# One-hot gating on VectorE, a final norm through PSUM, a 256-column last unit and a later norm sum in a two-block transformer kernel

## The reference, cut to what matters

```
def peer_ffn(...):            # first block: 128 x 128 product keys, 8 heads, top 16 each
    gate = softmax(top_s)     # the gate of each chosen (i, j) expert of a token
    act  = gelu(u[expert] . z)
    return sum(gate * act * v[expert])

def second_block(...):
    x = x + rmsnorm_2(y, g_post_mix)          # y: output of the mixing layers
    h = rmsnorm_2(x, g_pre_mlp)
    f = square(relu(h @ w_up)); f = f @ w_down     # 2048 -> 8192 -> 2048
    return x + rmsnorm_2(f, g_post_mlp)
rmsnorm(x, g) = x * rsqrt(mean(x * x) + eps) * g
```

## Time and profile before

| what | value |
|---|---|
| runs of the kernel before | 3310.08, 3315.99, 3294.74 us; median 3310.08 |
| profiled execution, its own time | 3305.67 us |
| its span, first to last instruction | 3303.8 us |
| TensorE busy | 3191.7 us (97%), 18206 matmuls |
| VectorE, ScalarE, GpSimd busy | 66%, 51%, 26% |
| mean granted clock of TensorE | 0.986 of full speed |

### The profile page before, as it was taken

How to read it: one execution, slowest core, us unless ns; L and a number is a source line. 1 busy time by engine, 2 the same in 40 slices (tenths; PEclk the granted TensorE clock), 3 DMA queues, 4 the chain that set the end, 5 groups by cost and what they waited for, 6 DMA issues and landing times.

```text
span 3303.8 us, 46932 instructions
## 1 busy us (share of the span) xinstructions
PE 3191.7 (97%) x18206; PEld 2781.5 (84%) x18206; DVE 2186.3 (66%) x2875; ACT 1681.1 (51%) x2625; POOL 870.7 (26%) x816
## 2 busy tenths in 40 slices
PE   7999989999999999999999998999998999999997
PEld 6788878888888888888888887888887788888886
DVE  7757998764655555564646579898675855555554
ACT  5554457644545444454545645555656444444453
POOL 1332344521313222231313434222342100000003
PEclk9999999999999999999999999999999999999999
DMA  6465546656565656565565554445665455565663
GB/s 211 149 198 181 179 154 217 236 184 211 187 214 186 211 186 214 186 210 186 193 208 185 185 184 140 159 155 184 190 189 170 153 189 189 190 191 189 190 189 127
DMA packets 177709, 615.35 MB, mean 186 GB/s; under 512 B 18128, under 2 KB 34896, under 8 KB 176080
## 3 DMA queue, kind: packets, MB, share of 16 engines
q1 hardware_dynamic: 157824, 572.59, 54.5%
q10 hardware_dynamic: 19664, 39.76, 3.4%
HBM read 593.41 MB, written 18.87 MB: 185 GB/s over the span
## 4 chain that ended last, share of the span: by engine, by line
PE 73%; DVE 16%; issue 4%; ACT 3%; POOL 3%; DMA 1%; ACTq 0%; POOLq 0%; DVEq 0%
PE G L399 48%; PE G L400 24%; DVE lo L995 7%; DVE CV L1291 2%; DVE oneB L1270 1%; POOL tS L1467 1%; ACT hi L627 1%; DVE tS L1001 1%; DVE oneA L1272 1%; ACT oneB L801 0%; DVE ZA L1314 0%; POOL X L1487 0%; POOL acc L1492 0%; ACT tA L634 0%; DMA X<-in_xT 0%
## 5 line engine op out<-in xcount | busy, mean ns | idle before, releaser
L399 PE MATMUL G<-ZA,hi 128*128 128x512 f32 x5120 | 1824.2, 401 | 29.2 <-DVE lo L995 11.3
L995 DVE TENSOR_TENSOR lo<-raw,hi 128x1024 fp32r<-128x1024 f32 x1088 | 1434.6, 1341 | 305.2 <-ACT hi L627 304.7
L400 PE MATMUL G<-ZA,lo 128*128 128x256 f32 x5120 | 1440.5, 281 | 0.0
L399 PE MATMUL G<-ZB,hi 128*128 128x512 f32 x3584 | 1257.2, 396 | 5.7 <-DVE ZB L1279 4.0
L399 PEld LDWEIGHTS G<-ZA,hi 128*128 128x128 f32 x5120 | 970.3, 190 | 261.2 <-DVE lo L995 13.3
L627 ACT ACTIVATE hi<-raw 128x1024 fp32r<-128x1024 f32 x1088 | 1106.5, 1051 | 46.2 <-DMA raw<-in_pv 30.7
L400 PE MATMUL G<-ZB,lo 128*128 128x256 f32 x3584 | 1003.3, 280 | 0.0
L400 PEld LDWEIGHTS G<-ZA,lo 128*128 128x128 f32 x5120 | 975.7, 191 | 0.6
L399 PEld LDWEIGHTS G<-ZB,hi 128*128 128x128 f32 x3584 | 672.7, 188 | 167.8 <-DVE lo L995 3.2
L634 ACT ACTIVATE tA<-G 128x256 f32<-128x256 f32 x560 | 212.5, 380 | 1001.7 <-PE G L400 998.1
L400 PEld LDWEIGHTS G<-ZB,lo 128*128 128x128 f32 x3584 | 676.8, 189 | 0.0
(11 more groups left out here) (264 smaller groups left out, 1383.2 us busy)
## 6 DMA issues: line engine op xcount, KB each, us to landing
raw<-in_pu SPq DMA_DIRECT2D x256, 512.0 KB, 3.6
raw<-in_pv SPq DMA_DIRECT2D x256, 512.0 KB, 3.6
raw<-in_w_in SPq DMA_DIRECT2D x192, 512.0 KB, 3.6
raw<-in_w_up SPq DMA_DIRECT2D x128, 512.0 KB, 3.6
raw<-in_w_down SPq DMA_DIRECT2D x128, 512.0 KB, 3.5
raw<-in_w_out SPq DMA_DIRECT2D x32, 512.0 KB, 3.5
raw<-in_wq SPq DMA_DIRECT2D x32, 512.0 KB, 3.5
g_scratch<-stage ACTq DMA_DIRECT2D x16, 1024.0 KB, 4.8
```

Of the source, the lines that this page charges most:

```text
L399: pe.matmul(G[:, 0:512], hi[h % NW][:, k % 8, :], Z[:, k, :], start=first, stop=False, skip_group_check=True)
L400: m = pe.matmul(G[:, 0:256], lo[h % NRAW][:, k % 8, :], Z[:, k, 0:256], start=False, stop=last, skip_group_check=True)
L995: dve.tensor_tensor(lo[r][:, :, :], raw[r][:, :].rearrange("p (k n) -> p k n", k=8), hi[w][:, :, :].bitcast(F32), ALU.subtract).then_inc(s ...
```

## The change

Four edits, and a renaming of semaphores: two pairs of semaphores for loads become one each.

1. In `one_hot(k)` VectorE itself multiplies the last four tokens of `oneB` by their gates, right behind `oneA` of the same k. GpSimd's instruction is gone. TensorE's second half of `spread(k)` waits on the new semaphore.
2. In the last unit (u = N-1) the product of `hi` with 512 columns becomes two with 256 columns into the same 256 columns of PSUM, so that one sum holds everything. ScalarE's copy and GpSimd's addition are left out, and VectorE adds Y to the bank directly.
3. At the end ScalarE copies the factor R1 to a PSUM bank, VectorE writes the products to two PSUM banks and adds them to X from there. VectorE has six pieces and GpSimd two.
4. `total` for the norm before the MLP stands behind unit M0+12 and not M0+10, and VectorE forms R3 in step M0+13.

```diff
@@ TensorE, product
-                pe.matmul(G[:, 0:512], hi[h % NW][:, k % 8, :], Z[:, k, :], start=first, stop=False, ...)
+                if u == N - 1:
+                    pe.matmul(G[:, 0:256], hi[h % NW][:, k % 8, :], Z[:, k, 0:256], start=first, stop=False, ...)
+                    pe.matmul(G[:, 0:256], hi[h % NW][:, k % 8, :], Z[:, k, 256:512], start=False, stop=False, ...)
+                else:
+                    pe.matmul(G[:, 0:512], hi[h % NW][:, k % 8, :], Z[:, k, :], start=first, stop=False, ...)
                 m = pe.matmul(G[:, 0:256], lo[h % NRAW][:, k % 8, :], Z[:, k, 0:256], start=False, stop=last, ...)
@@ TensorE, spread
-                        pe.wait_ge(s_ogp, k + 1)
+                        pe.wait_ge(s_ogd, k + 1)
@@ TensorE, loop
-                if u == M0 + 10:
+                if u == M0 + 12:
                     total(2, acc[0], None, (s_rss, 1)).then_inc(s_mean, 1)
@@ ScalarE, evac
-                    low(u)
+                    if u < N - 1:
+                        low(u)
...
                         act.activation(R1[:, :], MB[3][:, 0:256], ACT.Sqrt, ...).then_inc(s_root, 1)
+                        act.wait_ge(s_rcp, 7)
+                        act.activation(MB[2][:, 0:256], R1[:, :], ACT.Copy).then_inc(s_rps, 1)
@@ VectorE, evac
+                if u == N - 1 and part == 1:
+                    dve.wait_ge(s_mm, done(u))
+                    dve.tensor_tensor(Y[:, i, :], GB[BANK[u] % 4][:, 0:256], Y[:, i, :], ALU.add).then_inc(s_join, 1)
-                if st == "dn" and part == 1:
+                if st == "dn" and u < N - 1 and part == 1:
@@ VectorE, one_hot
+                dve.wait_ge(s_ohb, k + 1)
+                dve.tensor_tensor(oB[k % 2][:, 4:8, :], oB[k % 2][:, 4:8, :],
+                                  IJG[:, 2, 8 * k + 4:8 * k + 8].unsqueeze(2).broadcast_to([128, 4, 128]),
+                                  ALU.mult).then_inc(s_ogd, 1)
@@ VectorE, loop (the four instructions that form R3)
-                if u == M0 + 10:
+                if u == M0 + 13:
@@ VectorE, end
-            dve.wait_ge(s_rcp, 7)
-            for n in range(8):
-                k = slice(2 * n, 2 * n + 2)
-                if n not in (1, 4):
-                    dve.tensor_tensor(Y[:, k, :], Y[:, k, :], over(R1, 2), ALU.mult).then_inc(s_fd, 1)
-                if n not in (1, 4, 6):
-                    dve.wait_ge(s_fd, FD_OF[n] - 1)
-                    dve.tensor_tensor(X[:, k, :], X[:, k, :], Y[:, k, :], ALU.add).then_inc(s_fd, 1)
+            dve.wait_ge(s_rps, 1)
+            for n in range(0, len(OUT_D), 2):          # OUT_D = (0, 1, 2, 3, 4, 5)
+                for m in (n, n + 1):
+                    k = slice(2 * OUT_D[m], 2 * OUT_D[m] + 2)
+                    P = MB[m % 2][:, :].rearrange("p (k t) -> p k t", k=2)
+                    if n:
+                        dve.wait_ge(s_fd, m - 1)
+                    dve.tensor_tensor(P, Y[:, k, :], over(MB[2][:, 0:256], 2), ALU.mult).then_inc(s_fm, 1)
+                for m in (n, n + 1):
+                    ...
+                    dve.wait_ge(s_fm, m + 1)
+                    dve.tensor_tensor(X[:, k, :], X[:, k, :], P, ALU.add).then_inc(s_fd, 1)
@@ GpSimd
-                if st == "dn" and c and part == 1:
+                if st == "dn" and c and u < N - 1 and part == 1:
...
-                if 67 <= u < 83:
-                    for k in (2 * (u - 67), 2 * (u - 67) + 1):
-                        pool.wait_ge(s_ohb, k + 1)
...
-                        pool.tensor_tensor(oB[k % 2][:, 4:8, :], oB[k % 2][:, 4:8, :],
-                                           IJG[:, 2, 8 * k + 4:8 * k + 8].unsqueeze(2).broadcast_to([128, 4, 128]),
-                                           ALU.mult).then_inc(s_ogp, 1)
...
-            for n in (1, 4, 6):
+            for m, n in enumerate(OUT_P):              # OUT_P = (6, 7)
                 k = slice(2 * n, 2 * n + 2)
-                if n == 6:
-                    pool.wait_ge(s_fd, FD_OF[6])
-                else:
-                    pool.tensor_tensor(Y[:, k, :], Y[:, k, :], over(R1, 2), ALU.mult).then_inc(s_fp, 1)
-                    pool.wait_ge(s_fp, FP_OF[n] - 1)
+                pool.tensor_tensor(Y[:, k, :], Y[:, k, :], over(R1, 2), ALU.mult).then_inc(s_fp, 1)
+                pool.wait_ge(s_fp, 2 * m + 1)
                 pool.tensor_tensor(X[:, k, :], X[:, k, :], Y[:, k, :], ALU.add).then_inc(s_fp, 1)
```

More of the change, by code:

```diff
@@ L127 @@
 MIX_D = {0: 2, 1: 4, 3: 6, 5: 8, 7: 10}
-FD_OF = {0: 2, 2: 4, 3: 6, 5: 8, 6: 9, 7: 11}
-FP_OF = {1: 2, 4: 4, 6: 5}
+OUT_D, OUT_P = (0, 1, 2, 3, 4, 5), (6, 7)
+OUT_PAIRS = (0, 1, 6, 2, 3, 7, 4, 5)
 TAIL_END = [7, 13, 18, 22]
@@ L254, in build @@
         s_x = [sem(f"s_x{i}") for i in range(4)]
-        s_col, s_con, s_gaw, s_gxw, s_poolw, s_keys, s_mask, s_neg = (
-            sem(n) for n in ("s_col", "s_con", "s_gaw", "s_gxw", "s_poolw", "s_keys", "s_mask", "s_neg"))
+        s_col, s_con, s_gw, s_poolw, s_keys, s_mn = (
+            sem(n) for n in ("s_col", "s_con", "s_gw", "s_poolw", "s_keys", "s_mn"))
         s_st = [sem("s_st0"), sem("s_st1")]
@@ L281, in build @@
         s_sfs, s_sfe, s_sfn = sem("s_sfs"), sem("s_sfe"), sem("s_sfn")
-        s_ohb, s_oha, s_oga, s_ogp, s_spm, s_spr = (
-            sem(n) for n in ("s_ohb", "s_oha", "s_oga", "s_ogp", "s_spm", "s_spr"))
+        s_ohb, s_oha, s_oga, s_ogd, s_spm, s_spr = (
+            sem(n) for n in ("s_ohb", "s_oha", "s_oga", "s_ogd", "s_spm", "s_spr"))
         s_ag, s_gta, s_gl2, s_gm2, s_vx = (
@@ L297, in build @@
             sem(n) for n in ("s_mg", "s_u", "s_yg", "s_pmd", "s_pmp", "s_rsd", "s_rsp", "s_rsq", "s_rss", "s_rn"))
-        s_rl, s_dy, s_yd, s_fd, s_fp = (
-            sem(n) for n in ("s_rl", "s_dy", "s_yd", "s_fd", "s_fp"))
+        s_rl, s_dy, s_yd, s_rps, s_fm, s_fd, s_fp = (
+            sem(n) for n in ("s_rl", "s_dy", "s_yd", "s_rps", "s_fm", "s_fd", "s_fp"))
         def weights(u, p):
@@ L398, in product @@
                 Z = weights(u, p)[1]
-                pe.matmul(G[:, 0:512], hi[h % NW][:, k % 8, :], Z[:, k, :], start=first, stop=False, skip_group_check=True)
+                if u == N - 1:
+                    pe.matmul(G[:, 0:256], hi[h % NW][:, k % 8, :], Z[:, k, 0:256], start=first, stop=False, skip_group_check=True)
+                    pe.matmul(G[:, 0:256], hi[h % NW][:, k % 8, :], Z[:, k, 256:512], start=False, stop=False, skip_group_check=True)
+                else:
+                    pe.matmul(G[:, 0:512], hi[h % NW][:, k % 8, :], Z[:, k, :], start=first, stop=False, skip_group_check=True)
                 m = pe.matmul(G[:, 0:256], lo[h % NRAW][:, k % 8, :], Z[:, k, 0:256], start=False, stop=last, skip_group_check=True)
```

29 lines of the change are left out of this document (12 added, 17 removed).

## The result

The changed kernel takes 3288.14 us (median of 14 runs, 3280.05 to 3300.54), the kernel before 3302.67 us in the same session (14 runs, 3292.91 to 3318.61). The ratio is 0.9947, with a 95% interval from 0.9929 to 0.9964: 14.5 us less by the medians.

The account below looks back on a forecast made before the run. TensorE, busy 97% of the span, was taken as the bound. Terms -3.2 - 6.6 - 5.4 = -15.2 us gave 3290.5 us from the profiled run, 3294.9 from the median; forecast 3292 us, range 3281 to 3303.

Parts of the forecast that it names:

- Gates: Gate stage: VectorE takes over GpSimd's product; 3.2 us less over the eight light and eight other steps.
- The step's balance (+0.60 - 0.85): Each gate step: VectorE's extra product costs 0.60 us, and the 0.85 us `oneB` lost to GpSimd is saved; net -0.25.
- TensorE's cap: Eight light gate steps: TensorE has only 0.15 us of idle time left, so each gains 0.15 us and not 0.25.
- takes its turns with `lo` as before: Gate stage: GpSimd's remaining scaling and four quarter gates come earlier in its queue and meet `lo` as before; no change counted.
- Norm's sum: Norm before the MLP: the later sum removes TensorE's 4.03 us wait and the lower clock behind it; 6.6 us less.
- the wait comes back later: Rival at the norm: `lo` stock runs out, TensorE waits as long in M0+12, nothing gained; 3299 us, chance 0.13.
- End: Last unit and behind the last product: earlier join and VectorE operations not waiting for GpSimd; 5.4 us less.
- The twelve operations: VectorE's final operations through PSUM: none waits for GpSimd, 7.4 us where it was 12.29; 4.9 us less.
- The rule that a load overlaps a matmul only in other row groups: Last unit in three pieces: by this rule open weight loads would cost an estimated 1.7 us; the forecast took +0.1.
- `oneB` at 2.06 us: Rival in the gate stage: GpSimd was not what held `oneB`, every step gains 0.60 us of work; 3305.5 us, chance 0.08.
- Slower by an in-place product of 1.95 us: Rival in the gate stage: VectorE's product is caught by GpSimd or ScalarE, 31 us more in 16 steps; 3327 us, chance 0.03.
- The base: Middle starting time assumed for the kernel before, 3307.9 us, from which the rivals' times were counted.

Follow-up runs that it names:

- the run in which it reads along: Changed kernel, with GpSimd computing an unused 128x512 product from SBUF behind each `oneB` of the gate stage; 3310.34 us, light steps 10.57 us.

## Why the prediction was right, and where not

The time (3288.1 for 3292 us) is in the range. By stages the profile gains 15.6 us against 15.2 forecast, but 1.2 us of this are pace: the edits themselves are worth 2.6 (gates) + 6.65 (norm) + 5.67 us (end), 14.9 us.

- **Gates: right in kind, 0.6 us too much, and the agreement of 3.2 with the first table is luck.** Forecast -3.2 us. The table has -3.3 in the changed kernel, where 1.2 us are the quicker pace from join 90 to 101, and -3.5 alone, where 0.9 us are the shorter wait ahead of the first one-hot. The edit's own worth is 2.6 us. The step's balance (+0.60 - 0.85) is confirmed: heavy steps fell by 0.24 to 0.26 us. GpSimd's hold is shown by the run in which it reads along. Two steps of the prediction failed, and they partly cancel. The first is TensorE's cap: I let light steps gain 0.15 us because of one idle time between two rows of TensorE; they gained 0.243 us. That gap (0.27 us from start to start) was a little under the mean of the eight light steps, 0.30 us, where it is 0.12 now; and the row leaves out that the one-hot products themselves took 1.78 for 1.70 us. The second is "takes its turns with `lo` as before": GpSimd, freed of its products, comes to its quarter gate a step earlier, and meets `lo` once more inside the stage, +1.1 us. The steps gained 3.4 us, less 1.1 us for that one; behind the stage 0.4 us come back.
- **Norm's sum: right.** Forecast -6.6; -6.65 in the changed kernel and -6.66 alone. No wait, clock 1.00. The rival "the wait comes back later" is dead. In seven of the other runs the same code took 1.2 us less, which is the pace again.
- **End: right within 0.3 us.** Forecast -5.4, measured -5.67. The join was worth 1.22 us and the copy cost 0.42, as said. The twelve operations took 7.26 us (7.4 said; -5.0 and not -4.9). The last unit, from its first product's start to its last one's, took 5.63 us for 5.43 before: +0.2, and I had +0.1. The writes cost nothing, where I had +0.2: from the end of the last operation to the span's end it is 2.52 us, before 2.57. The weight loads of the last unit start 0.12 us apart, three to a tile, just as the products do, and are shown as 0.19 us each. The rule that a load overlaps a matmul only in other row groups (the Trainium skill, "TensorE: Matmul & The Clock Gate", "What overlaps and what doesn't") would have cost an estimated 1.7 us, and the 0.2 us measured has no room for it. GpSimd's four operations took 1.27 us each, not about 1 us, and were done first all the same.
- **Rivals.** `oneB` at 2.06 us: no, 1.21. Slower by an in-place product of 1.95 us: no, 0.68 us; but the run with GpSimd reading along shows the mechanism with its size, some 21 us when something holds it.
- **The base** of 3307.9 us was 5 us too high; before ran at 3302.67 us in the longer session. That, not a term, is the 4 us between forecast and result.

## What to carry to other kernels

Moving work off GpSimd pays by the turns that VectorE gets back, and only where GpSimd reads SBUF and VectorE has two SBUF inputs; so count who reads SBUF, not who is busy. A small pause in a busy engine may be another engine's only turn: before closing it, look who runs in it. Compare stages by landmarks when the whole time varies by more than the edit is worth, and put the first landmark right at the edited work: a wait ahead of it, and the pace behind it, made 2.6 us look like 3.5 and 3.3.
